# Expert rounds of a mixture of experts: gather and copies by the kind of the next round, and the extra tokens of two tiles taken together

## The chip, the cores and the metric

The kernel runs on one core of one Trainium2 chip. The metric is the device time of one execution in microseconds.

## The reference, cut to what matters

Two model blocks of two layers each run on 256 tokens of width 1024, all in fp32. The change lies in one part, the mixture of experts of the first block's second layer:

```
logits = h @ w_router + b_router
top_val, top_idx = top_k(logits, 2);  top_w = softmax(top_val)
gate = einsum(top_w, one_hot(top_idx, 8))
for e in range(8):
    out = out + gate[..., e:e+1] * ((silu(h @ w1[e]) * (h @ w3[e])) @ w2[e])
```

w1 and w3 are 1024 x 3584 per expert and w2 is 3584 x 1024. Everything before (Hyena filters, neighbourhood attention, a gated feed-forward layer, a Fourier layer) and after (retention, S5, two convolutional feed-forward layers) is untouched.

## The kernel before, in words

**Rounds.** The tokens of an expert are gathered, and the expert is computed in one or more rounds. A narrow round takes up to 64 tokens; a wide one takes up to 128 tokens and up to 32 more, the extras (`NARROW, WIDE, EXTRA = 64, P, 32`). `all_rounds` (L521) reads two counts from the routing and runs `n_first` narrow rounds in one loop, then `n_pairs` pairs of a narrow and a wide round in a second one. With these inputs there are two narrow rounds and three pairs: five narrow rounds and three wide ones. In a pair `j` is the pair's number; in the first loop it is `None`.

**Weights.** A round streams 42 tiles of 1 MB through a ring of seven slots. ACT issues the loads, four tiles ahead (`AHEAD = 4`): at tile i it waits on `tile_used` for tile i - 3 and issues the load of tile i + 4 (`load_ahead`). PE raises `tile_used` when it is done with a tile.

**A narrow round** (`narrow` in `moe_tensor`) multiplies in plain fp32. The tokens `XGF` (64 columns) are the stationary operand in two 64-column strips (L647 for w1 and w3, L683 for w2).

**A wide round** (`wide`) gets the accuracy of fp32 from three products of rounded parts. ACT copies a half tile to `w_high` (L881), DVE subtracts it from the tile to get `w_low` (L1094), and `product` (L718 to L720) multiplies low tokens by high weights, high by high and high by low, two column blocks per half: six matmuls. There are four buffers for halves (`SPLIT = 4`), so ACT may copy half n once half n - 4 is used (`used_wait`). The extras stay in plain fp32: `extra` multiplies the 32 extra tokens (`XGX`, `MHTX`) by the tile itself in the ring, in four 32-column strips of the array, each with a quarter of the output columns (L733 for w1 and w3, L730 for w2; the trace shows each fp32 matmul as two instructions). `tiles` (L737) sets the order of a step (w1, w3 or w2 of one chunk, two tiles, four halves): two products, the extras of the first tile, two products, the extras of the second tile. A round has seven chunks and so 21 steps. The order over chunks is w1(c), the transposes of the hidden values of chunk c - 1, w2(c - 2), w3(c). At the end DVE multiplies the result with the gates (L1137, L1139) and PE scatters it to the tokens' places (L780, L787).

**The gather for the next round** stands near the end of each round, after w3 of the last chunk: `gather` (L605) multiplies the activations `H` (stationary, 128x128) by the one-hot matrix `PM` (moving, 128 columns): 16 matmuls, 32 instructions. In the narrow round of a pair `gather_extra` (L630) follows, with 32 moving columns. Then ACT's `tokens_high` copies the first 64 columns in plain fp32 to `XGF` for a narrow round (L809) and all 128 rounded to `XGH` for a wide one (L811), and DVE's `tokens_low` subtracts to get `XGL` (L1032, L1033). All of this is done in every round, whichever kind comes next. PE waits on `xg_low` before a round, which `tokens_low` raises.

Of the kernel before, what the change touches and what calls it, by code (L numbers as in the profile page):

```python
# [12 lines left out]
ACT = mybir.ActivationFunctionType  # L13
# [3 lines left out]
P = 128  # L17
# [149 lines left out]
def build(nc, A, out):  # L167
    with ExitStack() as ctx:
# [5 lines left out]
        def sem(name):  # L174
            if name not in sems:
                sems[name] = ctx.enter_context(nc.semaphore(name))
            return sems[name]
# [86 lines left out]
        def bank(i, a=None):  # L264
            return PS[i][:, :] if a is None else PS[i][:, :].rearrange("p (a b) -> p a b", a=a)
# [313 lines left out]
        def moe_tensor(pe, mod_rows):  # L579
# [20 lines left out]

            def gather():

                for k in range(KD):
                    for t in range(TT):
                        mm = pe.matmul(PS[k // 4][:, P * (k % 4):P * (k % 4) + P], H[:, t, P * k:P * k + P], PM[:, t, :],  # L605
                                       start=t == 0, stop=t == TT - 1)
                mm.then_inc(sem("gather_done"), 1)
# [8 lines left out]
            pe.wait_ge(sem("route_ready"), 5)  # L616
            gather()
            pe.wait_ge(sem("pick_ready"), 1)
# [17 lines left out]
            def narrow(g, m, j):  # L636
# [15 lines left out]
                for s in range(BLOCK_STEPS):  # L652
# [4 lines left out]
                    if s == BLOCKS:  # L657
                        pe.wait_ge(sem("moe_silu"), g * MOE_CHUNKS + MOE_CHUNKS)
                        pe.wait_ge(sem("pick_ready"), g + 2)
                        gather()  # L660
                        if j is not None:
                            gather_extra()
# [40 lines left out]
            def wide(g, j):  # L703
# [33 lines left out]
                def tiles(kind, c, b, bx):  # L737

                    for h in range(2):
                        product(kind, c, 2 * h, b)  # L740
                        product(kind, c, 2 * h + 1, b)
                        extra(kind, c, h, bx)

                pe.wait_ge(sem("xg_low"), g + 1)
                for c in range(MOE_STEPS):
# [4 lines left out]
                    if c == MOE_CHUNKS:  # L750
                        pe.wait_ge(sem("moe_silu"), g * MOE_CHUNKS + MOE_CHUNKS)
                        pe.wait_ge(sem("pick_ready"), g + 2)
                        gather()
                    if 1 <= c <= MOE_CHUNKS:
# [44 lines left out]
        def moe_scalar(act, ch):  # L799
# [4 lines left out]
            for t in range(TT):  # L804
                ch.step(act.activation(PW[:, 1, t:t + 1], M8[:, t, 1:2], ACT.Exp, bias=PW[:, 0, t:t + 1]), sem("pair_exp"))

            def tokens_high():
                for i in range(2):
                    act.activation(XGF[:, 4 * i:4 * i + 4, :], bank(i, 4)[:, :, 0:NARROW], ACT.Copy)  # L809
                for i in range(2):  # L810
                    ins = act.activation(XGH[:, 4 * i:4 * i + 4, :], bank(i, 4), ACT.Copy)  # L811
                ins.then_inc(sem("xg_high"), 1)
# [6 lines left out]
            act.wait_ge(sem("gather_done"), 1)  # L819
            tokens_high()  # L820

# [9 lines left out]
            def narrow(g, _, j):  # L831
# [8 lines left out]
                for s in range(BLOCK_STEPS):  # L840
# [11 lines left out]
                    if s == BLOCKS:  # L852
                        act.wait_ge(sem("gather_done"), g + 2)
                        tokens_high()
                        if j is not None:
                            act.wait_ge(sem("extra_gathered"), 2 * j + 1)
                            act.activation(XGX, PS[5][:, 0:SEQ].rearrange("p (k n) -> p k n", k=KD), ACT.Copy).then_inc(sem("extra_x"), 1)
# [11 lines left out]
            def wide(g, j):  # L869
# [33 lines left out]
                for c in range(MOE_STEPS):  # L903
                    if c < MOE_CHUNKS:
                        split("w1", c)
                    if c >= 2:
                        split("w2", c - 2)
                        if c == MOE_CHUNKS:
                            used_wait(act, j, half_of("w3", MOE_CHUNKS - 1, 3))
                            act.wait_ge(sem("gather_done"), g + 2)  # L910
                            tokens_high()
                        silu(c)
                        hidden_high(c)
                    if c == 1:

                        split("w3", c, 0, 2)
                        hidden_high(c)
                        split("w3", c, 2, 4)
                    elif c < MOE_CHUNKS:
                        split("w3", c)  # L920
                    if c < 2:
                        silu(c)
# [6 lines left out]
        def moe_vector(dve, ch, mod_ready):  # L929
# [114 lines left out]
            mod_ready(sa, 2, 1, 5)  # L1044
            dve.wait_ge(sem("xg_high"), 1)
            tokens_low()

# [20 lines left out]
            def narrow(g, _, j):  # L1068
                begin_round(g)
                for s in range(BLOCKS):  # L1070
# [5 lines left out]
                    if s == 1:  # L1076
                        next_pick(g)
                dve.wait_ge(sem("xg_high"), g + 2)
                tokens_low()
                if j is not None:  # L1080
                    dve.wait_ge(sem("extra_gathered"), 2 * j + 2)
                    dve.tensor_copy(PGTX, PS[6][:, 0:SEQ])
# [4 lines left out]
            def wide(g, j):  # L1087
# [14 lines left out]
                for c in range(MOE_STEPS):  # L1102
# [14 lines left out]
                    if c >= 2:  # L1117
                        split("w2", c - 2)
                        if c == MOE_CHUNKS:
                            dve.wait_ge(sem("xg_high"), g + 2)  # L1120
                            tokens_low()
                        if c <= MOE_CHUNKS:
                            hidden_low(c - 1)
# [1729 lines left out]
```

## Time and profile before

| | |
|---|---|
| median of 3 runs | 2632.31 us (2630.09 to 2633.8) |
| the profiled execution | 2632.81 us |
| its span, first to last instruction | 2631.0 us |
| mean granted clock of TensorE | 0.977 |
| PE, DVE, ACT busy, share of the span | 93%, 48%, 32% |
| HBM read | 645.38 MB |

The page describes one execution. PE is the matmul part of TensorE, PEld its weight loads, which can overlap with matmuls; DVE is VectorE, ACT ScalarE, and ACTq stands for the DMA issues on ACT's queue. Line numbers are those of the kernel. "Idle before" tells how long an engine stood idle ahead of an instruction and what released it; "issue" is idle time in which it waited for nothing that the profile shows. The ends of matmuls are modelled, so starts are the better measure.

### The profile page before, as it was taken

What the parts mean: (1) busy time and instruction counts of PE and PEld (TensorE: products, weight loads), DVE (VectorE), ACT (ScalarE), POOL (GpSimd) and SP (SyncE); (2) the same over time, 40 slices, a digit from 0 to 9 for tenths busy, and PEclk for the clock granted to TensorE, in tenths of its full rate; (3) what the DMA queues carried; (4) which work ended last, traced back from release to release, by engine and by line L of the source; (5) the groups of instructions that cost most, each with busy time, mean ns of one, the idle gap of its engine ahead of it and who ended that gap; (6) DMA issues with size and microseconds to landing.
All of it is one profiled execution on the core that took longest, in us unless ns stands there. A gap on an engine that the chain in (4) does not pass through costs nothing.

```text
span 2631.0 us, 39062 instructions
## 1 busy us (share of the span) xinstructions
PE 2433.7 (93%) x15909; PEld 1648.6 (63%) x15909; DVE 1263.6 (48%) x1932; ACT 850.6 (32%) x1218; POOL 218.0 (8%) x247
## 2 busy tenths in 40 slices
PE   6998999999887889998999989999989998898998
PEld 2864769954322326772577436768857996654996
DVE  3306645532401005651366306757445777894664
ACT  2101634421000004540255105544434543102553
POOL 0401200001000000000000000000000008362000
PEclk9998999999999999999999999999999999999999
DMA  8727175567999998778977798757557655524452
GB/s 296 175 86 272 25 251 189 183 260 273 381 412 412 409 415 328 260 242 347 396 252 259 263 408 298 258 193 231 192 193 246 207 187 176 203 118 136 161 190 83
DMA packets 248167, 648.94 MB, mean 247 GB/s; under 512 B 12623, under 2 KB 102896, under 8 KB 225656
## 3 DMA queue, kind: packets, MB, share of 16 engines
q10 hardware_dynamic: 111760, 358.68, 36.3%
q1 hardware_dynamic: 130648, 275.51, 29.8%
q0 software_dynamic: 5584, 12.28, 2.4%
q8 instruction: 126, 2.06, 0.3%
q14 instruction: 49, 0.40, 0.0%
HBM read 645.38 MB, written 1.05 MB: 246 GB/s over the span
## 4 chain that ended last, share of the span: by engine, by line
PE 77%; DMA 14%; DVE 5%; issue 2%; POOL 1%; ACT 1%; ACTq 0%; SPq 0%; POOLq 0%; DVEq 0%
DMA ring<-in_moe_w 11%; PE bank L1552 6%; PE bank L718 5%; PE bank L1569 5%; PE bank L1570 5%; PE bank L1571 5%; PE bank L719 4%; PE bank L720 4%; PE bank L647 4%; PE bank L1580 4%; PE bank L1579 4%; PE bank L1581 4%; PE bank L733 3%; PE bank L683 3%; PE bank L1613 2%; PE bank L2006 2%
## 5 line engine op out<-in xcount | busy, mean ns | idle before, releaser
L1094 DVE TENSOR_TENSOR w_low<-ring,w_high 128x1024 fp32r<-128x1024 f32 x252 | 305.0, 1224 | 121.1 <-ACT w_high L881 120.6
L881 ACT ACTIVATE w_high<-ring 128x1024 fp32r<-128x1024 f32 x252 | 265.6, 1059 | 231.6 <-PE bank L720 191.7
L647 PE MATMUL bank<-ring,arena 128*64 128x512 f32 (+1 forms) x1280 | 267.3, 553 | 67.6 <-DMA ring<-in_moe_w 60.5
L2484 DVE TENSOR_TENSOR ring_low<-ring,up_high 128x1024 fp32r<-128x1024 f32 x186 | 226.7, 1276 | 113.6 <-ACT up_high L2123 113.4
L1569 PE MATMUL bank<-ht_low,up_high 128*128 128x256 f32 x960 | 270.9, 282 | 0.0
L647 PEld LDWEIGHTS bank<-ring,arena 128*64 128x64 f32 x1280 | 85.2, 138 | 244.7 <-DMA ring<-in_moe_w 129.5
L2123 ACT ACTIVATE up_high<-ring 128x1024 fp32r<-128x1024 f32 x186 | 182.6, 1046 | 84.0 <-PE bank L1581 72.7
L1075 DVE TENSOR_TENSOR HT<-HT,bank 128x512 f32<-128x512 f32 (+1 forms) x20 | 12.4, 621 | 371.1 <-PE bank L647 371.1
L1569 PEld LDWEIGHTS bank<-ht_low,up_high 128*128 128x128 f32 x960 | 180.2, 188 | 1.6 <-issue 0.8
L1570 PE MATMUL bank<-ht_high_cf_up,up_high 128*128 128x256 f32 x640 | 180.0, 281 | 0.0
L1571 PE MATMUL bank<-ht_high_cf_up,ring_low 128*128 128x256 f32 x640 | 178.0, 278 | 0.0
L1552 PE MATMUL bank<-HT,ring 128*128 128x256 f32 x704 | 157.3, 385 | 8.3 <-ACT HT L2098 3.6
L1552 PEld LDWEIGHTS bank<-HT,ring 128*128 128x128 f32 x704 | 135.6, 193 | 30.3 <-issue 7.4
L683 PE MATMUL bank<-ring,arena 128*64 128x512 f32 x560 | 132.6, 612 | 12.6 <-DMA ring<-in_moe_w 12.6
L718 PE MATMUL bank<-w_high,tokens_low 128*128 128x512 f32 x336 | 141.5, 421 | 2.8 <-ACT hidden_high L901 2.8
L720 PE MATMUL bank<-w_low,tokens_high 128*128 128x512 f32 x336 | 132.5, 394 | 0.0
L719 PE MATMUL bank<-w_high,tokens_high 128*128 128x512 f32 x336 | 132.4, 394 | 0.0
L1570 PEld LDWEIGHTS bank<-ht_high_cf_up,up_high 128*128 128x128 f32 x640 | 120.8, 189 | 0.1
L1571 PEld LDWEIGHTS bank<-ht_high_cf_up,ring_low 128*128 128x128 f32 x640 | 120.4, 188 | 0.0
L851 ACT ACTIVATE HT<-bank 128x512 f32<-128x512 f32 (+1 forms) x20 | 10.9, 544 | 335.0 <-PE bank L647 246.4
L1579 PE MATMUL bank<-up_high,hid_low 128*128 128x512 f32 x264 | 103.5, 392 | 1.3 <-DVE ring_low L2484 1.3
L1581 PE MATMUL bank<-ring_low,hid_high 128*128 128x512 f32 x264 | 104.3, 395 | 0.0
(429 smaller groups left out, 4285.9 us busy)
## 6 DMA issues: line engine op xcount, KB each, us to landing
ring<-in_moe_w ACTq DMA_DIRECT2D x340, 1024.0 KB, 11.6
ring<-in_w_ada SPq DMA_DIRECT2D x48, 1024.0 KB, 7.1
ring<-in_ada_w SPq DMA_DIRECT2D x48, 1024.0 KB, 4.9
ring<-in_ffn_w_up SPq DMA_DIRECT2D x44, 1024.0 KB, 5.1
ring<-in_ffn_w SPq DMA_DIRECT2D x33, 1024.0 KB, 5.2
ring<-in_ret_w_in SPq DMA_DIRECT2D x24, 1024.0 KB, 5.2
ring<-in_ffn_w_down SPq DMA_DIRECT2D x22, 1024.0 KB, 4.9
ring<-in_w_in SPq DMA_DIRECT2D x12, 1024.0 KB, 9.5
```

What stands on the lines that cost most here:

```text
L647: mm = pe.matmul(PS[b][64 * n:64 * n + 64, 0:cols], XGF[:, ks * h + k, :], w[:, k, cols * n:cols * n + cols], start=h + k == 0, stop=ks * ...
L683: mm = pe.matmul(PS[4][64 * n:64 * n + 64, :], MHTN[s % 2][:, b + k, 64 * group:64 * group + 64], w[:, k, BANK * n:BANK * n + BANK], start ...
L718: pe.matmul(o, low[:, k, :], w_high[:, cols], start=first, stop=False)
L719: pe.matmul(o, high[:, k, :], w_high[:, cols], start=False, stop=False)
L720: mm = pe.matmul(o, high[:, k, :], w_low[:, cols], start=False, stop=last)
L881: act.activation(WH[half % SPLIT][:, :], slot(moe_first + i)[:, HALF * (half % 2):HALF * (half % 2) + HALF], ACT.Copy)\
L1094: dve.tensor_tensor(out=WL[half % SPLIT][:, :], in0=slot(i)[:, HALF * (half % 2):HALF * (half % 2) + HALF], in1=WH[half % SPLIT][:, :], op ...
L1552: mm = pe.matmul(PS[b][:, SEQ * m:SEQ * m + SEQ], w[:, k, P * m:P * m + P], src[:, k, :], start=k == 0, stop=k == KD - 1)
L1569: pe.matmul(o, high, HT_LOW[:, k, :], start=k == 0, stop=False)
L1570: pe.matmul(o, high, HT_HIGH[part][:, k, :], start=False, stop=False)
L1571: mm = pe.matmul(o, low, HT_HIGH[part][:, k, :], start=False, stop=k == KD - 1)
L2484: dve.tensor_tensor(out=low_of(base + tile, q), in0=slot(base + tile)[:, HALF * q:HALF * q + HALF], in1=high_of(part, n), op=ALU.subtract) ...
```

## The change

A gather for a narrow round moves 64 columns of `PM`; one for a wide round moves 128. After it ACT makes only the copy that the next round reads, and DVE subtracts only ahead of a wide round. `xg_low` is raised by ACT's narrow copy in the one case and by DVE's subtraction in the other, and `xg_high` now counts only gathers for wide rounds. In a step of a wide round all four products come first, then the extras of both tiles; the first tile's `tile_used` is raised that much later.

```
-            def gather():
+            def gather(n):
...
-                        mm = pe.matmul(PS[k // 4][:, P * (k % 4):P * (k % 4) + P], H[:, t, P * k:P * k + P], PM[:, t, :],
-                                       start=t == 0, stop=t == TT - 1)
+                        mm = pe.matmul(bank(k // 4, 4)[:, k % 4, 0:n], H[:, t, P * k:P * k + P], PM[:, t, 0:n], start=t == 0, stop=t == TT - 1)
...
-            gather()
+            gather(NARROW)
...
-                        gather()
-                        if j is not None:
+                        if j is None:
+                            gather(NARROW)
+                        else:
+                            gather(P)
                             gather_extra()
...
                 def tiles(kind, c, b, bx):
 
+                    for q in range(4):
+                        product(kind, c, q, b)
                     for h in range(2):
-                        product(kind, c, 2 * h, b)
-                        product(kind, c, 2 * h + 1, b)
                         extra(kind, c, h, bx)
...
-                        gather()
+                        gather(NARROW)
...
+            def tokens_narrow():
+                for i in range(2):
+                    ins = act.activation(XGF[:, 4 * i:4 * i + 4, :], bank(i, 4)[:, :, 0:NARROW], ACT.Copy)
+                ins.then_inc(sem("xg_low"), 1)
+
             def tokens_high():
-                for i in range(2):
-                    act.activation(XGF[:, 4 * i:4 * i + 4, :], bank(i, 4)[:, :, 0:NARROW], ACT.Copy)
                 for i in range(2):
                     ins = act.activation(XGH[:, 4 * i:4 * i + 4, :], bank(i, 4), ACT.Copy)
                 ins.then_inc(sem("xg_high"), 1)
...
-            tokens_high()
+            tokens_narrow()
...
-                        tokens_high()
-                        if j is not None:
+                        if j is None:
+                            tokens_narrow()
+                        else:
+                            tokens_high()
...
-                            tokens_high()
+                            tokens_narrow()
...
-            dve.wait_ge(sem("xg_high"), 1)
-            tokens_low()
...
-                dve.wait_ge(sem("xg_high"), g + 2)
-                tokens_low()
                 if j is not None:
+                    dve.wait_ge(sem("xg_high"), j + 1)
+                    tokens_low()
...
-                        if c == MOE_CHUNKS:
-                            dve.wait_ge(sem("xg_high"), g + 2)
-                            tokens_low()
```

## Rows read from the trace of the kernel before

**Rows 1.** The page, part 1: busy time, share, instructions of each engine

```profile
PE 2433.7 (93%) x15909; PEld 1648.6 (63%) x15909; DVE 1263.6 (48%) x1932; ACT 850.6 (32%) x1218; POOL 218.0 (8%) x247
```

**Rows 2.** Table by stretch, expert stage: busy us of each engine, clock, DMA share, GB/s

```profile
790.00:893.00 103.00, 84.65 (x405) 28.28 (x402) 8.47 (x24) 6.84 (x13) 0.00 (x0) 1.00 1.02 412
...
1003.00:1186.80 183.80, 182.05 (x1727) 130.10 (x1723) 120.02 (x129) 97.95 (x115) 0.00 (x0) 1.00 0.77 265
...
1586.00:1770.00 184.00, 182.27 (x1728) 130.33 (x1727) 120.09 (x129) 97.73 (x115) 0.00 (x0) 1.00 0.71 245
```

**Rows 3.** The waits, 676 to 1775: who waited for whom, total, times, longest

```profile
ACT w_high L881 <- PE bank L720: 191.7, 221, 2.8
...
PEld bank L647 <- DMA ring<-in_moe_w: 129.5, 91, 2.2
...
PEld bank L718 <- DVE w_low L1094: 0.6, 3, 0.2
```

**Rows 4.** The waits again, same stretch: weight loads ahead of the extras

```profile
PEld bank L733 <- issue: 30.6, 84, 0.4
...
PEld bank L730 <- issue: 15.0, 42, 0.4
```

**Rows 5.** Timeline of a wide round, 1155 to 1161: start, duration, what

```profile
1155.41 1.08 PE L733 MATMUL bank<-ring,arena 128*32 128x128 f32 x32
...
1156.42 0.50 PE L718 MATMUL bank<-w_high,tokens_low 128*128 128x512 f32 x1
...
1156.76 0.39 PE L719 MATMUL bank<-w_high,tokens_high 128*128 128x512 f32 x1
...
1159.09 0.40 PE L720 MATMUL bank<-w_low,tokens_high 128*128 128x512 f32 x1
1159.41 0.81 PEld L733 LDWEIGHTS bank<-ring,arena 128*32 128x32 f32 x32 [0.37 <-issue]
```

**Rows 6.** Timeline of PE at a narrow round's end: one tile, 64 in a run

```profile
977.91 1.94 PE L647 MATMUL bank<-ring,arena 128*64 128x512 f32 x8 [0.62 <-DMA ring<-in_moe_w]
...
987.78 13.95 PE L683 MATMUL bank<-ring,arena 128*64 128x512 f32 x64
```

**Rows 7.** Timeline of the end of the first wide round

```profile
1179.85 1.07 PE L730 MATMUL bank<-ring,arena 128*32 128x256 f32 x16
1179.96 1.29 DVE L1137 TENSOR_TENSOR arena<-bank,AD 128x512 f32<-128x512 f32 x2 [6.03 <-PE bank L720]
...
1181.63 0.70 PE L780 MATMUL bank<-arena 128*128 128x512 f32 x1 [0.71 <-DVE arena L1139]
```

**Rows 8.** Timeline, wide rounds: load issue on ACT's queue, copy, subtraction, reaction to extras

```profile
1156.69 0.38 ACTq L554 DMA_DIRECT2D ring<-in_moe_w  x1
...
1170.23 1.06 ACT L881 ACTIVATE w_high<-ring 128x1024 fp32r<-128x1024 f32 x1 [1.54 <-PE bank L720]
...
1171.32 1.23 DVE L1094 TENSOR_TENSOR w_low<-ring,w_high 128x1024 fp32r<-128x1024 f32 x1 [1.20 <-ACT w_high L881]
...
1160.56 0.29 DVE L1115 TENSOR_TENSOR HT<-HT,bank 128x128 f32<-128x128 f32 x1 [0.27 <-PE bank L733]
```

**Rows 9.** Timeline of PE: a gather of 128 columns, one of 32 behind it

```profile
979.78 3.84 PE L605 MATMUL bank<-arena,H 128*128 128x128 f32 x32
983.46 3.66 PE L630 MATMUL bank<-arena,H 128*128 128x32 f32 x32
986.95 0.42 PE L633 MATMUL bank<-ident,arena 128*128 128x128 f32 x2
```

**Rows 10.** Timeline: what PE waited for before the first round; a copy of ACT

```profile
682.14 5.50 PE L623 MATMUL bank<-H,arena 128*128 128x512 f32 x8 [3.51 <-DVE MODR L2360]
...
984.20 1.09 ACT L811 ACTIVATE tokens_high<-bank 128x512 fp32r<-128x512 f32 x2
```

**Rows 11.** Table by stretch: DMA share at a gather and after a wide round

```profile
875.00:880.00 5.00, 5.00 (x33) 2.96 (x33) 1.29 (x2) 2.13 (x5) 0.00 (x0) 1.00 1.01 421
...
1185.00:1190.00 5.00, 1.69 (x17) 0.62 (x16) 3.08 (x5) 0.00 (x0) 0.00 (x0) 1.00 0.15 56
```

## The prediction

> **What bounds the kernel now.** I read the page first, for which engine is full: PE is busy in 93% of the span, DVE and ACT in half or less [rows 1]. An average over stages says nothing about an edit inside one, so next came the table by stretch over the expert stage (687.57 to 1770). It shows two kinds of round with two limits [rows 2]. In the narrow stretch shown (there are five narrow rounds) all DMA engines are busy, share 1.02 at 412 GB/s, and PE stands idle for 18 of 103 us. In the wide rounds (the first and the last of three are shown) PE is busy for 99% of the time, 182.05 of 183.80 us, and DMA stands at 0.71 to 0.77. The list of waits says the same: PE's weight loads wait 129.5 us for the ring in L647 alone, a line of the narrow rounds, while in wide rounds they wait 0.6 us in all for w_low; there it is ACT that waits for PE, 191.7 us [rows 3]. So a microsecond of PE's sequence counts in a wide round, and in a narrow one it must show up as DMA time to count.
>
> **The sum is made against the profiled execution**, 2632.81 us (span 2631.0 and 1.8 around it). That is 0.5 us above the median of the runs shown, 2632.31.
>
> **The extras, two tiles together.** A wide round has 21 steps (w1, w3 and w2 of seven chunks), each of two tiles: 42 blocks of extras, 126 in three rounds. The rows of the two extra lines bear it out: 84 starts after a gap in the weight loads for L733 and 42 for L730 [rows 4]. Now the switch, from the timeline of PE [rows 5]. Inside a run of products one starts every 0.232 us (1156.76 to 1159.09: 2.33 us in ten steps). Around a block of extras three intervals are longer:
> - last product to first extra, 1159.09 to 1159.41: 0.32, so 0.09 over;
> - first extra to next product, 1155.41 to 1156.42: 1.01. Steady work in it is less. Four 32-column strips run side by side, so 32 instructions are 8 in turn; one alone needs 128 columns twice at the 2.4 GHz that the granted clock of 1.00 means, 0.107 us, together 0.853. That leaves 0.16 in which PE empties;
> - the first product to the second, 1156.42 to 1156.76: 0.34, so 0.11 over (its weights were not loaded ahead; weight loads of L718 begin only at 1156.42).
>
> Together 0.35 us per visit. The change makes one visit of two, 63 times in three rounds: 63 x 0.35 = 22.2 us. It rests on the second block following the first at 0.853, which no row of the extras shows. The nearest rows are those of the narrow rounds, which work with half the strips: one tile of eight instructions alone takes 1.94 us, 64 of them in a run 13.95, which is 1.74 per tile [rows 6]. Joining removes 0.20 there, and the switches to and from products are not in that figure. Ends for the pair: 0.20 (12.6 us) from these rows, 0.37 (23.3 us) if the steady time is read from starts inside a block ((1.08 - 0.27) / 31 x 32 = 0.836). I take 0.35, because each of its three pieces is seen in the wide round itself.
>
> **The end of a wide round.** There the two blocks of extras follow the last product instead of one. There the extras start at 1179.85, DVE's two products for YE at 1179.96, taking 1.29 us beside them; then DVE does YEX, and the scatter L780 starts at 1181.63, 1.78 us after the extras' start [rows 7]. YEX with its reactions is what is left of it behind YE, 1.78 - 0.11 - 1.29 = 0.38 us, and 0.1 more if DVE's overlap is counted out: 0.48. With two blocks YEX must wait for both: 0.853 + 1.07 + 0.07 + 0.48 = 2.47 us, 0.69 later. But the extras start 0.853 + 0.35 = 1.2 us earlier, so the round gains 0.5 and not 0.35 here. Three times 0.15 more: 0.5 us. Sum so far 22.7.
>
> **What the late release costs.** The first tile of a step is given back only after all four products and its extras. ACT waits for that tile before it copies the halves that lie three tiles on, and behind this wait stand, in ACT's queue, the tile's load and two copies, and behind those DVE's two subtractions, for which PE waits. I walk it with rows of before, t = 0 where the next product would start after the step's last. Extras 1 start at 0.09 and end at 1.17; the next engine reacts 0.07 later (1160.49 to L1115 at 1160.56); load issue 0.38 and 0.11 to the copy: 1.73; copy 1.06: 2.79; subtraction from 2.82, 1.23 us: 4.05; 0.1 to PE: 4.15 [rows 5, 8]. PE wants this half after both extras (0.09 + 0.853 + 1.01 = 1.95), six products of the next step (0.34 + 5 x 0.232 = 1.50) and six more (1.39): 4.84. Slack 0.69 us. The half after it is ready at 5.35 and wanted at 6.23, slack 0.9. DVE's product for hidden (its smaller part 0.29) comes after these two in its queue and ahead of halves that PE wants 5 us later; the ACT silu and hidden copies likewise. So I price the wait at nothing; its cover is the 0.69 us. The tile's successor is asked for about 3 us later than now, and it is needed four tiles (15 us) on, with DMA a quarter idle: nothing.
>
> **Gather by kind.** Nine gathers (one per round and one ahead) have 32 instructions each; six of them now move 64 columns instead of 128. Does that shorten them? L605 with 128 columns starts at 979.78 and the next group, L630, at 983.46, 3.68 us; L630, the same instructions with only 32 columns, hands over after 3.49 [rows 9]. So the loads of 128x128 weights set the pace, and 64 columns lie between: 0 to 0.19 us per gather. Three of the six stand in wide rounds, where PE counts: 0 to 0.6, I take 0.3 us. The others lie in narrow rounds or ahead of the first, where DMA or DVE decides: nothing.
>
> The Trainium skill (TensorE: Matmul & The Clock Gate, "Part 3: Packing small matmuls — row/col tiling") says that LDWEIGHTS overlaps with matmuls in flight only where the row groups differ. By that rule load and stream would add up in the gather, and halving the columns would give back stream time as well. The rows do not bear it out, since 32 and 128 columns take the same; the sum by the rule is the second rival below.
>
> **Copies.** In six of nine hand-overs ACT drops its two high copies (1.09 us) and DVE its two subtractions; in the other three ACT drops the two narrow ones [rows 10]. In a wide round ACT's copy stands before hidden_high and the w2 halves, where PE does not wait; in a narrow one DMA is at 1.01 right through the gather and the copies (875 to 880) [rows 11]. Before the first round PE waited for DVE's L2360, not for the subtractions queued behind it [rows 10], and ACT's next load comes 1.1 us earlier there, worth at most that; I take nothing, since PE's start hangs on L2360. Nothing for all of these; if the covers failed, at most 1 us per round.
>
> **Does the gain survive?** After a wide round the ring fills while PE scatters and takes up the loop again: DMA drops to 0.15 in 1185 to 1190 [rows 11]. So the next narrow round starts with a full ring either way, and the wide round's gain is not handed back.
>
> Sum: 22.7 + 0.3 = 23.0, so 2632.8 - 23.0 = 2609.8; I say 2610.
>
> **Rivals.**
> 1. *The stall takes over (slower).* ACT's wait for the first tile of a step, in the wide round, makes w_low late. For: the slack is a sum of eight pieces. Against: w_low kept PE waiting only 0.6 us so far. The stall hits nearly every step. It decides from 0.69 + 0.35 = 1.04 us over my walk; at 1.5 over, each step loses 0.81 and gains 0.35: 63 x 0.46 = +29, 2662 us. Chance 0.04. A milder form, 0.1 to 0.3 us lost per step, or a narrow round that hands some back: 63 x 0.2 = 12.6 of the 23 lost, 2622 (2616 to 2628); chance 0.09.
> 2. *The narrow gather pays.* If stream and load added up, each gather would lose 32 x 0.053 = 1.7 us, in wide rounds three times: 5.1 us instead of 0.3, 2605. Rows 9 speak against it. This is the page's rule of above. Chance 0.05.
> 3. *The change doesn't do what it says.* If each block of extras paid the emptying by itself, whatever stands before it, joining would save almost nothing: 0 to 3 us, 2631. For: no row shows one block behind another. Against: the run of 64 in rows 6. Chance 0.06.
> 4. *My forecast*, 2610 (2606 to 2615): chance 0.76.
>
> **The numbers.** A measurement of this kernel can tell 0.2%, some 5 us, from no change. Faster by more: 0.76 + 0.05 + 0.09 = 0.90. Within: rival 3, 0.06. Slower: 0.04. The range reaches from the second rival, 2604, into the milder form of the first, 2619; the other end of the pair's price (12.6 us, 2620) is just outside.
>
> **What would show it.** L733 and L730 each with half as many starts behind a gap (42 and 21), blocks of 64 and 32 instructions in about 1.9 us, wide rounds 7.5 us shorter, narrow stretches unchanged, the gather still near 3.65 us. Wrong would be: PE waiting for w_low more than a few us in total, a block that still takes 2.0 us, or narrow stretches that grow.

## The result, and the profile after

The changed kernel takes 2614.98 us in the median of four runs (2611.32 to 2620.17) against 2633.06; the ratio is 0.9933 with a 95% interval of 0.9922 to 0.9945. A second set, of six runs, gave 2612.05 and 0.9926 (0.9912 to 0.9939). The forecast was 2610, inside a range of 2604 to 2619. The gain of 18 to 19 us is real. It is 4 to 5 us short of the 23 that were summed, by the medians: the interval of the first set (14.5 to 20.5 us gained) excludes 23, that of the second (16.1 to 23.2) just reaches it. The rest of this text is mostly about those 4 to 5.

The profiled execution took 2611.32 us, its span is 2609.5, against 2631.0. First the page's busy times, which answer to [rows 1]:

```profile
PE 2410.0 (92%) x15909; PEld 1656.3 (63%) x15909; DVE 1245.2 (48%) x1920; ACT 828.8 (32%) x1200; POOL 217.9 (8%) x247
```

As many matmuls as before, and 24 us less of busy PE. ACT and DVE have lost 18 and 12 instructions, the copies and subtractions that the next round did not need.

The timeline of PE in a wide round, two steps behind each other, as in [rows 5] (line numbers have moved: L734 and L731 are the extras, L719 to L721 the products):

```profile
1107.20 1.96 PE L734 MATMUL bank<-ring,arena 128*32 128x128 f32 x64
1109.09 0.50 PE L719 MATMUL bank<-w_high,tokens_low 128*128 128x512 f32 x1
1109.43 0.39 PE L720 MATMUL bank<-w_high,tokens_high 128*128 128x512 f32 x1
...
1114.54 0.39 PE L721 MATMUL bank<-w_low,tokens_high 128*128 128x512 f32 x1
1114.86 1.41 PE L734 MATMUL bank<-ring,arena 128*32 128x128 f32 x44
```

A block of 64 instructions hands over after 1.89 us, where two blocks took 1.01 each, and a whole step lasts 7.66 us (1107.20 to 1114.86) where two halves took 4.00 each. The 0.34 at the first product and the 0.32 ahead of the extras are as they were; there is one of each where there were two. That is 0.34 us per step. The waits of the expert stage show the same count, in total us, times, longest (answers to [rows 3, 4]):

```profile
ACT w_high L887 <- PE bank L734: 129.2, 39, 3.4
...
PEld bank L734 <- issue: 15.3, 42, 0.4
...
PEld bank L731 <- issue: 7.4, 21, 0.4
...
PEld bank L719 <- DVE w_low L1098: 1.2, 3, 0.4
```

The starts behind a gap fell from 84 and 42 to 42 and 21. ACT now waits mostly for the extras (L734, and L731 with 52.6 us) and little for the last product of a half (L721, 16.4 us, where L720 had 191.7): the late release is there. PE pays for it. The 1.2 us of waiting for w_low in three rounds, where it was 0.6, are one weight load per round, with 0.40 us of idle time ahead of it where a switch has 0.20 anyway:

```profile
1083.59 1.69 PEld L734 LDWEIGHTS bank<-ring,arena 128*32 128x32 f32 x64 [0.37 <-issue]
1085.67 0.19 PEld L719 LDWEIGHTS bank<-w_high,tokens_low 128*128 128x128 f32 x1 [0.40 <-DVE w_low L1098]
```

DVE is late there because it has other work in its queue, the `pick` for the next round (L1025 to L1034, 14 small instructions from 1081.09 to 1084.49):

```profile
1078.81 2.36 DVE L1098 TENSOR_TENSOR w_low<-ring,w_high 128x1024 fp32r<-128x1024 f32 x2 [2.52 <-ACT w_high L887]
1081.09 0.15 DVE L1025 COPY arena<-AD 128x1 f32 x1
...
1084.21 0.28 DVE L1034 TENSOR_SCALAR arena<-arena 128x128 f32<-128x128 f32 x1
1084.40 4.63 DVE L1098 TENSOR_TENSOR w_low<-ring,w_high 128x1024 fp32r<-128x1024 f32 x4
```

The gather, in the timeline of PE (answers to [rows 9]):

```profile
1155.86 3.79 PE L605 MATMUL bank<-arena,H 128*128 128x64 f32 x32
1159.48 0.28 PE L761 MATMUL bank<-ident,HT 128*128 128x128 f32 x1
```

3.62 us with 64 columns, where 128 columns took 3.68.

So far the forecast. What it did not have is the turn of the loop, where PE leaves a wide round and takes up the next narrow one. After, on PE, from the scatter (L781, L788) to the first tile of the next round (L646):

```profile
1176.03 3.70 PE L781 MATMUL bank<-arena 128*128 128x512 f32 x8 [0.55 <-DVE arena L1140]
1179.66 1.52 PE L788 MATMUL bank<-arena 32*128 32x256 f32 x16
1186.15 4.11 PE L646 MATMUL bank<-ring,arena 128*64 128x256 f32 x18 [4.98 <-issue]
```

Before, the same rows of the chain that ended last:

```profile
1181.63 3.70 PE bank L780 x8
1186.78 3.47 issue
1190.25 15.68 PE bank L647 x96
```

The idle time grew from 3.47 to 4.98 us, and at the second turn from 3.56 to 5.65. It is called "issue": the profile names no engine and no transfer that is waited for. The table by stretch tells what else went on then (after: busy us of PE, PEld, DVE, ACT, POOL, granted clock, DMA share, GB/s):

```profile
1180.00:1182.00 2.00, 1.09 (x16) 0.31 (x8) 0.76 (x2) 0.00 (x0) 0.00 (x0) 1.00 1.02 418
1182.00:1184.00 2.00, 0.00 (x0) 0.00 (x0) 2.00 (x4) 0.00 (x0) 0.00 (x0) 1.00 0.81 324
1184.00:1186.00 2.00, 0.00 (x0) 0.00 (x0) 0.33 (x1) 0.00 (x0) 0.00 (x0) 0.78 0.00 0
1186.00:1188.00 2.00, 1.85 (x10) 1.12 (x12) 0.00 (x0) 0.00 (x0) 0.00 (x0) 0.50 0.03 8
```

and the same moment before:

```profile
1185.60:1187.60 2.00, 1.09 (x16) 0.31 (x8) 0.76 (x2) 0.00 (x0) 0.00 (x0) 1.00 0.12 39
1187.60:1189.60 2.00, 0.00 (x0) 0.00 (x0) 2.00 (x4) 0.00 (x0) 0.00 (x0) 1.00 0.00 0
```

Before, DMA was nearly quiet when PE stopped; now 1 MB of ring loads still runs through the first half of PE's pause.

The list of DMA queues of the same stretches has one more row than the kernel's own loads: queue 8, of the kind that the profile calls "instruction", moves one packet of 16 KB in every such pause (queue, kind: packets, MB, share). After, from the start of the pause to 1183.38, and from there to PE's restart:

```profile
q10 hardware_dynamic: 231, 0.91, 100.9%
...
q10 hardware_dynamic: 31, 0.07, 6.8%
q8 instruction: 1, 0.02, 2.4%
```

Before, from 1187.17, 0.4 us into the pause, to PE's restart:

```profile
q8 instruction: 1, 0.02, 2.6%
```

So the packet starts 0.4 us into the pause before and 2.2 us into it after, when 0.91 MB of ring loads has passed, and PE restarts 3.1 and 2.8 us behind the packet's start. In all 14 profiles, 28 pauses of 3.05 to 6.12 us, PE restarts 2.6 to 3.2 us behind the start of this packet. What grows is the time until the packet starts: 0.4 to 1.0 us in pauses of at most 3.6 us, 2.0 to 3.3 us in those of 4.8 us and more. What PE stands still for at the turn is, by this, its next instructions. The profile does not link the packet to PE by name; the link is this constancy. Inside a round the queue moves such a packet every 8 to 16 us or so, and PE does not stop for it there.

The restart falls into a stretch of low clock in both kernels (0.50, which is 1.2 GHz), and in the changed one it is longer. The table by stretch for the 5 us behind the first pause, before and after, has 0.66 and 0.50 in the clock's column; behind the second it is 0.66 and 0.52:

```profile
1190.25:1195.25 5.00, 5.00 (x32) 3.17 (x34) 0.00 (x0) 0.00 (x0) 0.00 (x0) 0.66 0.15 24
...
1186.15:1191.15 5.00, 5.00 (x24) 2.97 (x26) 0.00 (x0) 0.00 (x0) 0.00 (x0) 0.50 0.08 10
```

Why the loads are later is in ACT's timeline, after:

```profile
1166.76 0.39 ACTq L554 DMA_DIRECT2D ring<-in_moe_w  x1
1167.26 2.01 ACT L887 ACTIVATE w_high<-ring 128x1024 fp32r<-128x1024 f32 x2 [3.19 <-PE bank L731]
1174.12 1.95 ACTq L567 DMA_DIRECT2D ring<-in_moe_w  x3
```

ACT's last two copies of the round wait 3.19 us for the extras of the step before (L731). Then ACT itself turns to the next round and issues three loads from 1174.12, 1.9 us ahead of the scatter; before, this was 1176.13, 5.5 us ahead of it:

```profile
1176.13 5.38 ACTq L567 DMA_DIRECT2D ring<-in_moe_w  x3
```

The last of the three issues ends about as long ahead of PE's pause in both kernels, 5.3 us before (1181.51 to 1186.78) and 5.1 after (1176.07 to 1181.18). What differs is the data: the three loads now go out close behind each other, and the last MB of them is moved in the pause.

### The profile page after: what moved, and what is told of

It is laid out like the page before. It is cut to its first block, busy times and chain, and to the rows that moved or that the text cites. A ratio compares the mean times of both kernels' runs of the same rounds, so it can differ in the third digit from the quotient of the medians.

```text
span 2609.5 us, 39030 instructions
## 1 busy us (share of the span) xinstructions
PE 2410.0 (92%) x15909; PEld 1656.3 (63%) x15909; DVE 1245.2 (48%) x1920; ACT 828.8 (32%) x1200; POOL 217.9 (8%) x247
## 4 chain that ended last, share of the span: by engine, by line
PE 76%; DMA 14%; DVE 6%; issue 2%; ACT 1%; POOL 1%; ACTq 0%; SPq 0%; DVEq 0%; POOLq 0%
DMA ring<-in_moe_w 11%; PE bank L1553 6%; PE bank L1570 5%; PE bank L1571 5%; PE bank L1572 5%; PE bank L719 5%; PE bank L721 4%; PE bank L720 4%; PE bank L646 4%; PE bank L1581 4%; PE bank L1582 4%; PE bank L1580 4%; PE bank L684 3%; PE bank L734 3%; PE bank L1614 2%; PE bank L2007 2%
## 5 line engine op out<-in xcount | busy, mean ns | idle before, releaser
L1098 DVE TENSOR_TENSOR w_low<-ring,w_high 128x1024 fp32r<-128x1024 f32 x252 | 296.0, 1221 | 135.9 <-ACT w_high L887 135.9
L646 PE MATMUL bank<-ring,arena 128*64 128x512 f32 (+1 forms) x1280 | 268.8, 557 | 70.6 <-DMA ring<-in_moe_w 60.0
L887 ACT ACTIVATE w_high<-ring 128x1024 fp32r<-128x1024 f32 x252 | 254.9, 1057 | 237.8 <-PE bank L734 129.2
L646 PEld LDWEIGHTS bank<-ring,arena 128*64 128x64 f32 x1280 | 85.6, 140 | 248.8 <-DMA ring<-in_moe_w 129.1
L719 PE MATMUL bank<-w_high,tokens_low 128*128 128x512 f32 x336 | 136.9, 408 | 3.2 <-ACT hidden_high L907 2.8
L721 PE MATMUL bank<-w_low,tokens_high 128*128 128x512 f32 x336 | 132.7, 395 | 0.0
L720 PE MATMUL bank<-w_high,tokens_high 128*128 128x512 f32 x336 | 132.5, 394 | 0.0
```

Of the source, the lines that this page charges most:

```text
L646: mm = pe.matmul(PS[b][64 * n:64 * n + 64, 0:cols], XGF[:, ks * h + k, :], w[:, k, cols * n:cols * n + cols], start=h + k == 0, stop=ks * ...
L719: pe.matmul(o, low[:, k, :], w_high[:, cols], start=first, stop=False)
L720: pe.matmul(o, high[:, k, :], w_high[:, cols], start=False, stop=False)
L721: mm = pe.matmul(o, high[:, k, :], w_low[:, cols], start=False, stop=last)
L887: act.activation(WH[half % SPLIT][:, :], slot(moe_first + i)[:, HALF * (half % 2):HALF * (half % 2) + HALF], ACT.Copy)\
L1098: dve.tensor_tensor(out=WL[half % SPLIT][:, :], in0=slot(i)[:, HALF * (half % 2):HALF * (half % 2) + HALF], in1=WH[half % SPLIT][:, :], op ...
```

## The experiments

Every kernel stood beside runs of the kernel before on the same chip. All wide rounds, turns and narrow rounds below are those of one profiled execution each. The table has what the expectations speak of, read from each profile; the first number is the time from the scatter of a narrow round (L700, before L699) to that of the wide round behind it, which holds the whole wide round; "turn" is the idle time ahead of the first narrow tile after the first and second wide round; "narrow" is the time from the scatter of a wide round to that of the narrow one behind it.

| kernel | wide, us | turn, us | narrow, us | ratio, 95% interval |
|---|---|---|---|---|
| before | 179.01 | 3.47, 3.56 | 111.75, 113.39 | 1 |
| changed | 171.58 | 4.98, 5.65 | 112.12, 114.89 | 0.9933 (0.9922 to 0.9945) |
| changed, again | 171.59 | 5.25, 5.30 | 112.87, 112.35 | 0.9926 (0.9912 to 0.9939) |
| extras only | 171.61 | 5.56, 5.42 | 115.23, 112.49 | 0.9942 (0.9928 to 0.9956) |
| gather and copies only | 178.97 | 3.07, 3.46 | 111.31, 111.32 | 1.0003 (0.9993 to 1.0013) |
| last step by tile | 172.16 | 4.79, 4.87 | 114.00, 112.73 | 0.9938 (0.9922 to 0.9955) |
| last two steps by tile | 172.56 | 3.05, 3.25 | 111.17, 113.54 | 0.9937 (0.9925 to 0.9950) |
| second to last by tile | 172.00 | 3.48, 3.25 | 110.15, 109.34 | 0.9927 (0.9915 to 0.9940) |
| all w2 steps by tile | 174.27 | 3.11, 3.33 | 107.99, 112.82 | 0.9932 (0.9916 to 0.9948) |
| four visits per step | 193.47 | 3.30, 3.60 | 113.05, 110.66 | 1.0173 (1.0156 to 1.0190) |
| loads held back at the turn | 171.58 | 3.56, 3.45 | 120.69, 119.09 | 0.9988 (0.9980 to 0.9997) |
| loads two tiles later | 171.37 | 5.02, 5.45 | 111.87, 114.86 | 0.9919 (0.9904 to 0.9935) |
| w2 and w3 in one visit | 169.70 | 5.19, 5.17 | 115.62, 114.46 | 0.9914 (0.9898 to 0.9929) |
| the same, last two by tile | 170.71 | 5.42, 6.12 | 113.30, 114.77 | 0.9925 (0.9912 to 0.9938) |

The first column repeats within 0.08 us in the rounds of any one kernel, so it settles small terms which the ratio, with an interval of 2 to 4 us to either side, cannot.

**The changed kernel once more.**

> The changed kernel itself, for the spread of its time. Theory (extras joined save 0.35 us per visit in the wide rounds, and after a wide round PE takes up the loop later, because the ring's last loads now fall into that moment): 2615 us in the median, 0.993 of before; wide rounds 171.6 us from the first product's stretch to L781, and the idle time ahead of the first L646 after a wide round 5.0 to 5.7 us instead of 3.5. Rival (the missing 5 us are another chip state or chance): 2610, and gaps that differ between executions without reference to the load traffic.

2612.05 us, six runs, with turns of 5.25 and 5.30 us. The long turn is no chance of one execution. The median came out nearer to the rival's 2610 than to the 2615 expected: two sets of the same kernel differ by 3 us, and totals of this kernel say no more than that.

**One half of the change at a time.** First only the order of the extras:

```
                 def tiles(kind, c, b, bx):
 
+                    for q in range(4):
+                        product(kind, c, q, b)
                     for h in range(2):
-                        product(kind, c, 2 * h, b)
-                        product(kind, c, 2 * h + 1, b)
                         extra(kind, c, h, bx)
```

> Only the order of products and extras is changed; gather and copies stay as before. Theory: all of the gain comes from here, 0.993 of before, within 2 us of the whole change. Rival (the narrower gather and the dropped copies carry part): more than 3 us slower than the whole change.

Then gather and copies as in the change, with the order of extras as before:

> Only gather and copies go by the kind of the next round; the order of extras stays as before. Theory: 0 to 1 us faster than before, ratio 0.9995 to 1.0, the gather 3.7 us long with 64 columns as with 128. Rival (loads and streams add up in the gather): 5 us faster, ratio 0.998, the gather near 2 us.

The extras alone bring the wide round from 179.01 to 171.61 us; gather and copies alone to 178.97. The sum of both, 7.44, is what the whole change shows, 7.43. In total the first gives 0.9942, 4 us behind the whole change measured beside it. That is outside the 2 us expected and on the rival's side (more than 3 us), but the two intervals overlap, the wide rounds are the same to 0.03 us, and the second kernel leaves nothing for the rival. The second changes nothing that can be measured. Its gather, in PE's timeline of this run:

```profile
1165.73 3.79 PE L605 MATMUL bank<-arena,H 128*128 128x64 f32 x32
1169.35 0.28 PE L761 MATMUL bank<-ident,HT 128*128 128x128 f32 x1
```

That is 3.62 us. The rival with loads and streams that add up, about 2 us, is out.

**The price of a visit.** The kernel with more visits does half a tile's extras after each product:

```
-                    for q in range(4):
-                        product(kind, c, q, b)
-                    for h in range(2):
-                        extra(kind, c, h, bx)
+                    for q in range(4):
+                        product(kind, c, q, b)
+                        extra(kind, c, q // 2, bx, q % 2)
```

> The changed kernel, but with more visits instead of fewer: half a tile's extras after each product, four visits per step, 84 per wide round, each with half the instructions. Theory (each visit costs 0.35 us whatever its length): 42 more visits per wide round than before, 3 x 42 x 0.35 = +44 us against before, 2677 us, ratio 1.017; a visit of half a tile near 0.58 us. Rival (the price grows with the work in a visit, not with their number): within 5 us of before.

2678.32 us, ratio 1.0173. The wide round grew by 14.46 us for 42 more visits, 0.344 us each. The kernel with the extras joined and nothing else saved 7.40 (179.01 less 171.61) for 21 fewer, 0.352 each. The same price in both directions, with half the work in a visit and with twice as much, rules out that it grows with the work (the rival had the kernel within 5 us of before). The timeline of PE of this run:

```profile
1100.12 0.65 PE L736 MATMUL bank<-ring,arena 128*32 128x128 f32 x16
1100.70 0.50 PE L719 MATMUL bank<-w_high,tokens_low 128*128 128x512 f32 x1
1101.04 0.39 PE L720 MATMUL bank<-w_high,tokens_high 128*128 128x512 f32 x1
```

16 instructions take 0.58 us, 32 take 1.01 and 64 take 1.89: 0.43 to 0.44 for each 16 and 0.15 to 0.16 once, and around them 0.34 and 0.32 as ever.

The kernel with w2 by tile keeps 14 joined steps:

```
                 def tiles(kind, c, b, bx):
 
+                    if kind == 'w2':
+                        for h in range(2):
+                            product(kind, c, 2 * h, b)
+                            product(kind, c, 2 * h + 1, b)
+                            extra(kind, c, h, bx)
+                        return
                     for q in range(4):
```

> The changed kernel, but all w2 steps take their extras tile by tile; w1 and w3 steps keep them joined: 14 of 21 visits saved per wide round. Theory (0.35 us per saved visit, the same for every kind): wide rounds 2.6 us longer than in the changed kernel, 7.8 us over three, less what the earlier release at the loop's turn gives back (2 to 4 us): 0.995 of before. Rival (the price lies in the w2 form with its 256 columns): almost the whole gain gone, 0.999.

Wide rounds are 2.69 us longer than in the changed kernel, 2.6 expected. With the 0.58 us that the last step costs (below) it is 0.35 for each of the other six visits: no kind of step differs. But the total stayed at 0.9932 where 7.8 us of lost saving, less 2 to 4, had put 0.995, just beyond the interval's end. Here the turns are 3.1 and 3.3 us, which accounts for what was allowed for and not for more; why this kernel is 4 to 5 us faster than expected is open.

**Whether the late release costs in the wide round.** ACT issues each load two tiles later, behind the copies:

```
                         if half % 2 == 0:
                             tile_landed(act, g, i)
-                            load_ahead(g, now, after, i)
+                            if i >= 2:
+                                load_ahead(g, now, after, i - 2)
...
+                for i in range(NT - 2, NT):
+                    load_ahead(g, now, after, i)
```

> The changed kernel, but in wide rounds ACT issues each load two tiles later, so that its copies of a tile never stand behind the release of the tile of the step before. Theory (the late release is covered by slack and costs nothing in a wide round): wide rounds unchanged at 171.6 us, total within 3 us of the changed kernel. Rival (the release held up w_low here and there): wide rounds shorter by 0.5 us or more.

171.37 against 171.58, so the release cost 0.21 us per round, less than the rival's 0.5: the waits for w_low fall back from 1.2 to 0.6 us over the three rounds, which is that amount. The 0.6 that is left is no wait, as it is three gaps of 0.20, the gap of every switch. The cover was real but not complete. With this, four tiles can be put in one visit, w2 and w3 of a chunk:

```
+                    if kind == "w2" and c < MOE_CHUNKS - 2:
+                        return
+                    if kind == "w3" and c >= 2:
+                        for h in range(2):
+                            extra("w2", c - 2, h, 6)
                     for h in range(2):
                         extra(kind, c, h, bx)
```

> Loads two tiles later as in the run before, and the extras of w2 and w3 of a chunk taken together, in one visit of four tiles: 16 visits per wide round instead of 21. Theory (0.35 us per visit): 3 x 5 x 0.35 = 5.3 us faster than the changed kernel, 2610 us, unless the release is now too late. Rival (the release of four tiles at once holds up the copies for the next step): wide rounds as long as in the changed kernel or longer, with waits for w_low of 0.3 us or more per chunk.

The wide round loses another 1.67 us, five visits of 0.334. The total is 2609.66 us, ratio 0.9914, the lowest of all; its interval overlaps with that of the changed kernel.

**The turn.** Five kernels bear on it. Only the last step (w2 of the last chunk) by tile:

> The changed kernel, but the very last step of a wide round (w2 of the last chunk) takes its extras tile by tile as before, so that its first tile is released early. Theory (late loads hold up PE at the loop's turn): the gap after a wide round falls back from 5.0 to 5.7 us to about 3.5, twice; the step itself loses 0.5 us, three times; in all 0 to 3 us faster than the whole change. Rival (the gap has nothing to do with the loads): gap as in the changed kernel, and 1.5 us slower than it.

A miss: the turns stay at 4.8 and 4.9 us, and the total of 2613.36 is 1.3 us above the changed kernel's beside it, both as the rival had it. But this kernel did not move the loads as it was meant to. ACT's timeline of this run shows why:

```profile
1165.61 2.01 ACT L893 ACTIVATE w_high<-ring 128x1024 fp32r<-128x1024 f32 x2 [3.19 <-PE bank L731]
1172.57 17.75 ACTq L567 DMA_DIRECT2D ring<-in_moe_w  x5
```

ACT's last copies still wait 3.19 us, since what they wait for is the first tile of the step before the last. ACT is 2.4 us ahead of the scatter (at 1174.95). So the second to last step was taken back too, and then it alone (the condition is `kind == 'w2' and c >= MOE_CHUNKS - 2`, and `c == MOE_CHUNKS - 2`):

> The changed kernel, but the last two steps of a wide round (w2 of the last two chunks) take their extras tile by tile. In the run with only the last step so, ACT's last copies still stood behind the release of the step before. Theory (the turn of the loop is slow where the loads of tiles 4 to 6 fall into PE's own turn): gap after a wide round back at 3.1 to 3.6 us, twice; wide rounds 172.5 us, 0.9 longer each; narrow rounds after wide ones about 2 us shorter in the mean; in all 0 to 3 us faster than the changed kernel. Rival (the gap follows the joined w1 and w3 steps): gap above 4.5 us.

> The changed kernel, but only the second to last step of a wide round (w2 of the sixth chunk) tile by tile. Theory (that step's early release is what lets ACT do its last copies and its own turn before PE's): ACT's first load after the turn 4 us or more ahead of the scatter instead of 1.9, gap under 4.5 us, wide rounds 171.9 us. Rival (the last step's release decides, whose tiles the loads 5 and 6 wait for): gap 5 us as in the changed kernel.

Both bring the turn back to 3.05 to 3.48 us. In the second, the loads go out at 1173.35, 4.6 us ahead of the scatter (at 1177.95); the timelines of ACT, with PE's last row:

```profile
1168.50 1.06 ACT L893 ACTIVATE w_high<-ring 128x1024 fp32r<-128x1024 f32 x1 [0.32 <-PE bank L721]
1173.35 4.64 ACTq L567 DMA_DIRECT2D ring<-in_moe_w  x3
...
1186.58 3.71 PE L646 MATMUL bank<-ring,arena 128*64 128x256 f32 x18 [3.48 <-issue]
```

It is the second to last step that counts, not the last. The narrow rounds behind the wide ones take 112.4 and 109.7 us in the mean, where the two profiles of the changed kernel have 113.5 and 112.6; about 2 us less was expected of the first. In the total neither can be told from the changed kernel: 2613.74 and 2610.06 us. Expected was a gain of 0 to 3 us for the first.

Last, the direct test. The order is the changed one, ACT's turn is as late as ever, but the loads are held back:

```
                 def block_ahead(i):
 
-                    tile_wait(act, g, i + AHEAD - RING)
+                    tile_wait(act, g, max(0, i + AHEAD - RING))
```

> The changed kernel, but ACT holds the loads of tiles 4 to 6 of a narrow round back until PE has used its first tile, so that no ring load runs while PE takes up the loop again. Theory (load traffic holds up PE's turn): gap 3.0 to 3.6 us instead of 5.0 to 5.7; the narrow rounds then run 5 to 8 us longer each, since these loads are late and DMA bounds them, so the whole is 20 to 40 us slower than the changed kernel. Rival (the gap has another cause, as ACT's own turn or the semaphores): gap 5 us or more although DMA is idle.

The table by stretch of this run in PE's pause, and the first tile behind it:

```profile
1186.00:1188.00 2.00, 0.00 (x0) 0.00 (x0) 2.00 (x4) 0.00 (x0) 0.00 (x0) 1.00 0.04 8
...
1189.30 3.01 PE L646 MATMUL bank<-ring,arena 128*64 128x256 f32 x14 [3.56 <-issue]
```

With DMA quiet the turn is 3.56 and 3.45 us, in an otherwise unchanged order. Holding the loads back takes away their issue on ACT's queue as well as their traffic, but the issues were over about 5 us ahead of the pause with and without the change. Together with the instruction packet, which here starts 0.4 us into the pause, this shows load traffic as the cause of the longer pause. The narrow rounds pay for the late loads with 120.69 and 119.09 us; the total rose by some 15 us against the changed kernel and not by the 20 to 40 expected, as only the two narrow rounds behind wide ones carry it and each costs 7; the others keep their 107.1 and 110.7 us.

The last kernel joins w2 and w3 and takes the last two steps by tile:

> The run with loads two tiles later and the extras of w2 and w3 in one visit, and the last two steps of a wide round tile by tile. Theory: wide rounds 170.6 us, gap 3.1 to 3.6 us, narrow rounds after wide ones 2 us shorter in the mean: 2607 to 2610 us, the fastest of all. Rival (nothing comes back from the gap, the narrow rounds being bound by DMA): 2612 us, 3 us slower than without the old steps.

2609.68 us, but the turns are 5.42 and 6.12: with the loads two tiles later, ACT issues the last of them at the round's end, and its own turn comes late again (first load at 1175.48, scatter at 1177.08). So the expected turn did not come, and with 0.9925 against 0.9914 the combination shows no gain over its sibling.

## Why the prediction was right, and where 4 to 5 us went

**Visits, 22.2 us: right.** 0.352 us each downwards and 0.344 upwards against 0.35. The assumption that no row showed, a second block at 0.853 behind the first, came out at 0.88 (1.89 less 1.01).

**End of a wide round, 0.5 us: right in kind.** Taking the last step back costs 0.58 us (172.16 against 171.58) where 0.5 was said; PE's wait for DVE ahead of the scatter also fell, from 0.71 to 0.55 us.

**Late release, nothing: nearly.** It costs 0.21 us per round, 0.6 in all. The walk gave 0.69 us of slack and no stall, and this holds for all steps but one in a round. It had DVE's subtractions and its product for hidden in the queue, but not the 3.4 us of `pick` for the next round, which stand there once per round; behind them w_low comes 0.2 us late. The 0.6 us of waiting that the prediction took from [rows 3] were three ordinary gaps of 0.2 us, so PE did not wait for w_low at all.

**Gather, 0.3 us: small, as said.** It is 0.04 to 0.06 us each, so 0.1 to 0.2. The rule that loads overlap only with other row groups, which the Trainium skill states (TensorE: Matmul & The Clock Gate, "Part 3: Packing small matmuls — row/col tiling"), does not describe this gather: halving its columns left 3.62 of 3.68 us. By itself the rule leaves out what the same section also allows, a load into a background weight buffer.

**Copies, nothing: right.** 1.0003.

**"Does the gain survive?": this step failed.** It said that the ring fills in the pause either way, so the wide round's gain is kept. It looked at whether the loads would be done in time, not at what they run beside. The prediction's own sign of being wrong, narrow stretches that grow, came: 112.12 and 114.89 us where 111.75 and 113.39 were. The late release moves ACT's last two copies, these move ACT's own turn, and this moves three loads of 1 MB later and closer together, so that the last MB runs in PE's pause and PE's instruction packet starts behind it.

What this costs can be estimated in three ways. The two pauses grew by 3.6 us together (1.51 and 2.09), and by 3.5 in the second profile of the changed kernel. Over all kernels with a pause of at most 3.6 us (six kernels, twelve turns, without the one whose loads are held back) the narrow round behind it took 111.4 us in the mean, from 107.99 to 113.54; over those with 4.8 us or more (seven kernels, fourteen turns) 113.7, from 111.87 to 115.62. The difference of 2.3 us, twice, is 4.6. The ranges overlap, so the figure is a mean and no more: in the two profiles of the changed kernel itself these narrow rounds were 1.9 and 0.1 us longer than before, taken together. The totals, which do not rest on single executions, agree with it. The gain by the ratio falls short of three times the wide round's gain by 4.4 us in the mean of the seven kernels with long pauses (1.6 to 6.9), and by 0.8 in the five with short ones (from 2.8 short to 3.7 over; the kernel before and the one with held loads are left out). The difference is 3.6 us.

Three wide rounds of 7.43 are 22.3; less 3.6 to 4.6 it makes 17.7 to 18.7, and the two sets of runs had 18.1 and 19.3.

The profiled execution alone would have hidden it. It gained 21.5 us: 22.3 in the wide rounds, less 1.9 behind them and 1.8 in the first pair's narrow round, which has no long pause ahead of it and takes 109.0 to 112.3 us over all the kernels, and 2.9 more because the part after the experts happened to be shorter in it (863.3 against 866.2 us from the last scatter to the end, and 862.5 to 869.7 over all the kernels, which share that code).

**Rivals.** Of the slower one, a stall on w_low, 0.2 us per round came true. The third, that each block pays for itself, is ruled out by 1.89 us for 64 instructions. The milder form of the first had "a narrow round that hands some back", with 12.6 us; that is what happened, at about a third of its price, for a reason that it did not give.

Left open: why PE restarts 2.6 to 3.2 us behind the start of a packet that itself takes about 1 us, why ACT's own turn grew (below), and how the 3.6 to 4.6 us divide between the pause and the clock behind it. No version is shown to be faster than the changed one (0.9933 and 0.9926). The lowest ratios are 0.9914, w2 and w3 in one visit, and 0.9919, loads two tiles later; the intervals of both overlap with that of the changed kernel. What the last kernel aimed at, more joined steps and an early turn of ACT at once, was not reached.

## What to carry to other kernels

Count visits, not instructions, where an engine changes between two kinds of work: here a visit costs 0.35 us in whatever way the work is cut, and the same price can be read from three intervals of one timeline before anything is built. And when a buffer is released later, follow the release to the end of the stage and past it: it cost little where it was looked for, under the products, and most where the loop turns. Where a pause there is called "issue", ask the list of DMA queues whether a packet of the kind "instruction" starts late in it. A total that moves by 3 us between two sets cannot settle such terms; the length of one stage, which repeats within 0.1 us, can.

## What was not expected of the hardware

PE's pause at the turn of the loop lasts 3.1 to 3.6 us when DMA is quiet by the time it begins or soon after, and 4.8 to 6.1 us when ring loads run into it. In the changed kernel the pause began at 1181.18, the instruction packet started at 1183.38 when the loads ran out (DMA moved nothing from 1184 to 1186), and PE came back at 1186.15. So 16 KB of instructions started 2.2 us into the pause, behind 0.91 MB of data, where before they started 0.4 us into it.

ACT's turn is longer there as well: 4.85 us from its last copy's end (1169.27) to its next load (1174.12), against 3.46 before (1172.67 to 1176.13). It, too, has a packet of the kind "instruction", 8 KB on queue 14, and its next load follows 3.1 to 3.5 us behind the packet's start in every kernel but the one whose loads are held back. The packet starts 0.3 us behind the last copy before and 1.6 us in the changed kernel; why is not shown.

Behind the pause PE works at the lower of its two clock levels (0.50, 1.2 GHz) for a while, in the kernel before as in the changed one, so the pause costs more than its length. In the changed kernel it took 24 instructions in the first 5 us at 0.50, where before it took 32 at 0.66.
